# First expert gathers fed by GpSimd, rows in two column halves, one weight step moved ahead, and a residual write left out

## The reference

```python
def hierarchical_moe(hn, w_router_group, w_router_expert, w_gate, w_up, w_down):
    g_probs = softmax(t @ w_router_group); g_w, g_idx = top_k(g_probs, 1)
    e_in_group = (t @ w_router_expert)[group g_idx]          # 4 groups of 8 experts
    top_l, top_i = top_k(e_in_group, 2); weights = softmax(top_l) * g_w
    for e in range(32):
        hid = silu(t @ w_gate[e]) * (t @ w_up[e])            # 2048 -> 256
        out = out + (hid @ w_down[e]) * comb[:, e:e + 1]     # 256 -> 2048
```

## Time and profile before

| what | value |
|---|---|
| median of the runs | 2225.68 us (2225.47 to 2228.48, 3 runs) |
| the profiled execution's own time | 2228.09 us |
| its span | 2226.3 us |
| PE busy | 2156.8 us, 97% of the span |
| DVE busy | 1315.8 us, 59% |
| ACT busy | 900.7 us, 40% |
| POOL busy | 15.6 us, 1% |
| share of the chain that ended last | PE 83%, DMA 10%, DVE 4%, ACT 2% |
| moved | 520.49 MB, 234 GB/s over the span |

### The profile page before, as it was taken

One profiled execution on the slowest core, in us unless ns is written; L12 is line 12 of the kernel. 1 busy time (PEld: TensorE's weight loads), 2 busy tenths in 40 slices (PEclk: granted clock), 3 DMA queues, 4 the chain that ended last, 5 costly groups with the idle time before them and its releaser, 6 DMA issues.

```text
span 2226.3 us, 31966 instructions
## 1 busy us (share of the span) xinstructions
PE 2156.8 (97%) x12035; PEld 1699.3 (76%) x12035; DVE 1315.8 (59%) x1788; ACT 900.7 (40%) x1188; POOL 15.6 (1%) x30
## 2 busy tenths in 40 slices
PE   9999999999899888999999999999999999999998
PEld 8888888555445445888888888888888888888886
DVE  7797566422222224766667665777777777764443
ACT  4564455411111112554435454554434343433342
POOL 1000000000000000000000000000000000000000
PEclk9999999999999999999999999999999999999999
DMA  7765455899999998556654545546656556565653
GB/s 252 216 202 152 133 187 209 351 419 421 421 421 421 421 421 341 179 175 214 211 173 162 162 157 185 168 154 189 189 188 188 188 188 188 188 209 191 196 191 131
DMA packets 283474, 520.49 MB, mean 234 GB/s; under 512 B 22065, under 2 KB 194145, under 8 KB 258529
## 3 DMA queue, kind: packets, MB, share of 16 engines
q1 hardware_dynamic: 280560, 507.60, 65.2%
q0 software_dynamic: 2800, 11.34, 1.5%
HBM read 514.63 MB, written 7.36 MB: 234 GB/s over the span
## 4 chain that ended last, share of the span: by engine, by line
PE 83%; DMA 10%; DVE 4%; ACT 2%; issue 1%; SPq 0%; DVEq 0%; ACTq 0%
PE acc L723 30%; PE acc L744 24%; PE acc L747 12%; DMA mw<-in_w_expert_up 7%; PE ps L1168 5%; PE acc L1243 3%; DMA mw<-in_w_expert_gate 2%; DVE wlo L1977 1%; PE tp L832 1%; DMA mw_late<-in_w_expert_up 1%; PE ps L900 1%; PE tp L1126 1%; PE tp L1116 0%; PE ps L847 0%; PE tp L915 0%
## 5 line engine op out<-in xcount | busy, mean ns | idle before, releaser
L1977 DVE TENSOR_TENSOR wlo<-raw,whi 128x1024 fp32r<-128x1024 f32 x572 | 675.7, 1220 | 210.7 <-ACT whi L1461 206.2
L744 PE MATMUL acc<-xhl,whi 128*128 128x512 f32 x2496 | 790.6, 398 | 1.6 <-DVE wlo L1977 0.7
L1461 ACT ACTIVATE whi<-raw 128x1024 fp32r<-128x1024 f32 x572 | 582.1, 1053 | 351.9 <-DMA raw<-in_w_down 132.4
L747 PEld LDWEIGHTS acc<-xhl,wlo 128*128 128x128 f32 x2496 | 468.9, 188 | 110.8
L747 PE MATMUL acc<-xhl,wlo 128*128 128x256 f32 x2496 | 490.8, 278 | 0.0
L744 PEld LDWEIGHTS acc<-xhl,whi 128*128 128x128 f32 x2496 | 381.4, 189 | 5.8 <-issue 3.0
L1168 PE MATMUL ps<-mw,xg_turn 128*64 128x256 f32 x1536 | 177.2, 384 | 29.0 <-DMA mw<-in_w_expert_gate 22.1
L1168 PEld LDWEIGHTS ps<-mw,xg_turn 128*64 128x64 f32 x1536 | 112.0, 138 | 97.6 <-issue 27.0
L723 PE MATMUL acc<-whi,xhl 128*128 128x512 f32 x480 | 155.8, 395 | 0.0
L723 PE MATMUL acc<-whi,ah 128*128 128x512 f32 x336 | 130.7, 389 | 0.0
L723 PE MATMUL acc<-wlo,ah 128*128 128x512 f32 x336 | 130.7, 389 | 0.0
(11 more groups left out here) (457 smaller groups left out, 2394.7 us busy)
## 6 DMA issues: line engine op xcount, KB each, us to landing
raw<-in_w_in SPq DMA_DIRECT2D x352, 256.0 KB, 3.0
raw<-in_w_up SPq DMA_DIRECT2D x352, 256.0 KB, 2.9
mw<-in_w_expert_up SPq DMA_DIRECT2D x52, 1024.0 KB, 17.2
mw<-in_w_expert_gate SPq DMA_DIRECT2D x50, 1024.0 KB, 18.0
mw<-in_w_expert_down SPq DMA_DIRECT2D x48, 1024.0 KB, 18.2
raw<-in_w_down SPq DMA_DIRECT2D x176, 256.0 KB, 3.3
raw<-in_w_out SPq DMA_DIRECT2D x128, 256.0 KB, 3.2
raw<-in_w_ple_gate SPq DMA_DIRECT2D x64, 256.0 KB, 3.4
```

The costliest lines, as they stand in the source:

```text
L744: pe.matmul(out(ct).rearrange("p (m n) -> p m n", m=2), wh[:, ct * P:ct * P + P], ahl[:, :, k, :], start=first, stop=False, skip_group_che ...
L747: mm = pe.matmul(out(ct)[:, S:2 * S], wl[:, ct * P:ct * P + P], ahl[:, 0, k, :], start=False, stop=last, skip_group_check=True)
L1461: act.activation(whi[:, m % RING, :], raw[:, m % RING, :], ACT.Copy).then_inc(hi_ready, 1)
L1977: dve.tensor_tensor(wlo[:, m % RING, :], raw[:, m % RING, :], whi[:, m % RING, :], ALU.subtract).then_inc(lo_ready, 1)
```

## The change

ScalarE no longer makes `x_hi` for the first eight column groups. It writes the scaled rows themselves (`scaled_rows`) into space of `upb` that is still free, the first tile ahead of its wait for the router product. GpSimd copies them to `x_hi` (rounding to float32r) and subtracts to get `x_lo`. `x_hi` and `x_lo` hold eight column groups instead of sixteen; the second half is written over the first once eight gathers are done, by ScalarE (`high_rows`) and VectorE (`low_rows(1)`, now behind `slots_ready`). TensorE does eight gathers ahead of the first `gate_up`, followed by twelve small products without a use (`run_in`), and the other eight after the second `gate_up`. LATE no longer overlaps the rows, so step 6 goes there and is requested directly after step 2. The write of `h` to DRAM goes, and the overflow branch starts from `xp` and `g_pack` instead. Two scratch tiles move.

```diff
-OV_PE, OV_ACT, OV_DVE = 10, 1, 9
-OV_X = KT // 2
+OV_PE, OV_ACT, OV_DVE = 13, 1, 10
+OV_X = 1
+OV_IN = 96
 MAX_OVER = 7
+RUN_IN_MOE = 12
 EARLY, LATE = 4, 5
-PLACE = [EARLY, 0, 1, 2, 3, EARLY, 0, LATE, 1, 2, 3]
-PLACE += [PLACE[6 + (s - 6) % 5] for s in range(len(PLACE), N_STEPS)]
+PLACE = [EARLY, 0, 1, 2, 3, EARLY] + [(LATE, 0, 1, 2, 3)[s % 5] for s in range(N_STEPS - 6)]
...
-        junk_ra = at("junk_ra", 57, [P, 1536])
-        junk_la = at("junk_la", 63, [P, 512])
+        junk_ra = at("junk_ra", 26, [P, 1536])
+        junk_la = at("junk_la", 18, [P, 512])
...
-        x_lo = at("x_lo", 33, [P, TT, KT, P], F32R)
-        x_hi = at("x_hi", 49, [P, TT, KT, P], F32R)
+        upb_rows = at("x_scaled_rows", 73, [P, TT, D])
+        x_lo = at("x_lo", 33, [P, TT, KT // 2, P], F32R)
+        x_hi = at("x_hi", 41, [P, TT, KT // 2, P], F32R)
+        ov_w = at("ov_w", 33, [P, KT, P])
+        ov_gt = at("ov_gt", 65, [P, PACK // P, S])
+        ov_hid = at("ov_hid", 69, [P, PACK // P, 256])
+        x_part = [upb_rows[:, 1 - t, 1024:2048].rearrange("p (k q) -> p k q", k=8) for t in range(TT)]
...
@@ -470,8 +472,6 @@
                 earlier = [q for q in range(step) if PLACE[q] == r]
                 if earlier:
                     sp.wait_ge(w_used, earlier[-1] + 1)
-                elif r == LATE:
-                    sp.wait_ge(t_done, KT)
                 else:
                     sp.wait_ge(chunk_used, ND_MOE if r in (2, 3) else ND_MOE - 4)
                 m = 4 // len(sources)
@@ -479,14 +479,17 @@
                     dst = ring_w[r][:, m * j:m * j + m, :].rearrange("p a b -> p (a b)")
                     sp.dma_start(dst, w[e, :, m * c * CHUNK:m * (c + 1) * CHUNK]).then_inc(w_in_g[r], 16)
 
+            def pair_step(g, i):
+
+                c = i if g else FIRST_PAIR[i]
+                load_step(STEPS * g + i, [((wgp, wup)[c // 2], e, c % 2) for e in (2 * g, 2 * g + 1)])
+
             for g in range(PAIRS):
                 for i in range(4):
-                    c = i if g else FIRST_PAIR[i]
-                    load_step(STEPS * g + i, [((wgp, wup)[c // 2], e, c % 2) for e in (2 * g, 2 * g + 1)])
+                    if STEPS * g + i != STEPS:
+                        pair_step(g, i)
                     if g == 0 and i == 2:
-                        sp.wait_ge(acc_free[0], MIX_END[0])
-                        sp.wait_ge(acc_free[1], MIX_END[1])
-                        sp.dma_start(h_d, h[:, :, :]).then_inc(h_out, 16)
+                        pair_step(1, 0)
                 for j in range(2):
...
+            for t in range(TT):
+                pool.wait_ge(x_scaled, t + 1)
+                pool.tensor_copy(x_hi[:, t, :, :], x_part[t]).then_inc(xh_ready, 1)
+                pool.wait_ge(xh_ready, t + 1)
+                pool.tensor_tensor(x_lo[:, t, :, :], x_part[t], x_hi[:, t, :, :], ALU.subtract).then_inc(xl_ready, 1)
...
                 for m in range(2 * TT):
-                    mm = pe.matmul(o[:, :], x_k[m // TT][:, m % TT, kt, :], g_pack[:, m % TT, :], start=m == 0,
+                    mm = pe.matmul(o[:, :], x_k[m // TT][:, m % TT, kt % 8, :], g_pack[:, m % TT, :], start=m == 0,
                                    stop=m == 2 * TT - 1, skip_group_check=True)
...
-                    pe.wait_ge(ov_x, TT)
-                    for k in range(KT // 2):
-                        if k >= 2:
-                            pe.wait_ge(ov_act, k - 1)
-                        for j in range(2):
-                            for t in range(TT):
-                                x_t = h_was[:, t, :].rearrange("p (q k) -> p k q", k=KT)
-                                mm = pe.transpose(tp[k % 2][:, j * S + t * P:j * S + (t + 1) * P], x_t[:, 2 * k + j, :], ident[:, :])
-                        mm.then_inc(ov_pe, 1)
-                    pe.wait_ge(ov_act, KT // 2)
+                    for q in range(PACK // P):
+                        for t in range(TT):
+                            mm = pe.transpose(tp[q // 2][:, q % 2 * S + t * P:q % 2 * S + (t + 1) * P],
+                                              g_pack[:, t, q * P:(q + 1) * P].bitcast(F32), ident[:, :])
+                    mm.then_inc(ov_pe, 1)
+                    pe.wait_ge(ov_act, 2)
                     with pe.Fori(0, count) as i:
-                        for m in range(2):
-                            pe.wait_ge(ov_in, i * 48 + (16 * m + 16))
-                            for ht in range(2):
+                        for m in range(4):
+                            o = ((ps[0], ps[1]), (acc[1][:, 0:512], acc[1][:, 512:1024]))[m // 2]
+                            pe.wait_ge(ov_in, i * OV_IN + (16 * m + 16))
+                            for q in range(PACK // P):
+                                c = q % 2 * 256 + m % 2 * P
                                 for k in range(KT):
-                                    mm = pe.matmul(ps[m][:, ht * S:(ht + 1) * S], ov_w[:, k, ht * P:(ht + 1) * P], xT[:, k, :],
+                                    mm = pe.matmul(o[q // 2][:, c:c + P], xp[:, k, q * P:(q + 1) * P], ov_w[:, k, :],
                                                    start=k == 0, stop=k == KT - 1, skip_group_check=True)
                         pe.wait_ge(ov_dve, i * OV_DVE + 1)
+                        for m in range(2):
+                            for q in range(PACK // P):
+                                mm = pe.matmul(tp[0][:, m * S:(m + 1) * S], ov_hid[:, q, m * P:(m + 1) * P], ov_gt[:, q, :],
+                                               start=q == 0, stop=q == PACK // P - 1, skip_group_check=True)
+                        mm.then_inc(ov_pe, 1)
...
             pe.wait_ge(packed_ready, 1)
-            for kt in range(11):
+            for kt in range(8):
                 gather(kt)
+            run_in(RUN_IN_MOE)
...
                 gate_up(g, 0)
                 gate_up(g, 1)
                 if g == 0:
-                    for kt in range(11, KT):
+                    for kt in range(8, KT):
                         gather(kt)
...
+            act.wait_ge(n_inv, rows.n)
+
+            def high_rows(half, t):
+
+                act.activation(x_hi[:, t, :, :], h[:, t, :].rearrange("p (q k) -> p k q", k=KT)[:, 8 * half:8 * half + 8, :], ACT.Copy,
+                               scale=rstd2[:, 1, t:t + 1]).then_inc(xh_ready, 1)
+
+            def scaled_rows(t):
+
+                act.activation(x_part[t], h[:, t, :].rearrange("p (q k) -> p k q", k=KT)[:, 0:8, :], ACT.Copy,
+                               scale=rstd2[:, 1, t:t + 1]).then_inc(x_scaled, 1)
+
+            scaled_rows(0)
             act.wait_ge(rt_mm, 1)
             act.activation(lgT[:, :], ps[0][:, 0:S], ACT.Copy).then_inc(rt_copy, 1)
...
-            act.wait_ge(n_inv, rows.n)
-            for half in range(2):
-                ks = slice(8 * half, 8 * half + 8)
-                for t in range(TT):
-                    act.activation(x_hi[:, t, ks, :], h[:, t, :].rearrange("p (q k) -> p k q", k=KT)[:, ks, :], ACT.Copy,
-                                   scale=rstd2[:, 1, t:t + 1]).then_inc(xh_ready, 1)
-                embedded(half)
+            scaled_rows(1)
+            embedded(0)
+            embedded(1)
             act.wait_ge(rt_read, 2)
             act.activation(g_e[:, :, :], g_sh[:, :, :], ACT.Exp).then_inc(rt_e, 1)
             act.wait_ge(rt_read, 3)
             act.activation(r_s[:, 7, :], r_s[:, 6, :], ACT.Exp).then_inc(rt_e, 1)
+            act.wait_ge(xl_ready, TT)
             embedded(2)
             embedded(3)
...
                 copies(xg_first[half], first, slice(8 * half, 8 * half + 8))
+                if half == 0:
+                    act.wait_ge(t_done, 8)
+                    for t in range(TT):
+                        high_rows(1, t)
...
-            def low_rows(half):
-
-                ks = slice(8 * half, 8 * half + 8)
-                for t in range(TT):
-                    dve.wait_ge(xh_ready, TT * half + t + 1)
-                    dve.scalar_tensor_tensor(x_lo[:, t, ks, :], h[:, t, :].rearrange("p (q k) -> p k q", k=KT)[:, ks, :],
-                                             rstd2[:, 1, t:t + 1], x_hi[:, t, ks, :], ALU.mult, ALU.subtract).then_inc(xl_ready, 1)
-
-            low_rows(0)
             each = [P, TT, N_EXPERTS]
             dve.wait_ge(rank_mm, 1)
...
-            low_rows(1)
+            def low_rows(half):
+
+                for t in range(TT):
+                    dve.wait_ge(xh_ready, TT * half + t + 1)
+                    dve.scalar_tensor_tensor(x_lo[:, t, :, :], h[:, t, :].rearrange("p (q k) -> p k q", k=KT)[:, 8 * half:8 * half + 8, :],
+                                             rstd2[:, 1, t:t + 1], x_hi[:, t, :, :], ALU.mult, ALU.subtract).then_inc(xl_ready, 1)
+
...
             dve.sem_inc(slots_ready, 1)
+            low_rows(1)
...
-                if g == 1:
-                    dve.wait_ge(h_out, 16)
```

(3 more changed lines are left out.)

62 lines of the change are left out of this document (29 added, 33 removed).

## The result

| | before | after |
|---|---|---|
| median | 2226.84 us (2225.47 to 2228.77, 7 runs) | 2234.77 us (2231.39 to 2238.01, 7 runs) |
| the profiled execution, its span | 2228.09, 2226.3 us | 2231.39, 2229.6 us |

The changed kernel is slower: ratio 1.0035, 95% interval [1.0026, 1.0044], some 8 us. The forecast of 2225.5 us was wrong, and the time lies above its range. The profiled execution of the changed kernel is the shortest of its runs, that of before lies above its median, so the two traces differ by only 3.3 us.

A forecast was written before the change was run, and what follows sets the result against it. Bound by TensorE's chain from the router to its seventh weight step, then the weight stream. 2.2 us won less 2.06 paid left 0.1: 2228.0 us, or 2225.5 as median; own range 2222.6 to 2227.4, with rivals to 2231.9.

The forecast's parts named there:

- (3): GpSimd's four row instructions beside the router: about 8 us, done at 388.4 us, within a cover of 12.9 us, costing nothing.
- rival A: VectorE's two-input router operations stand still while GpSimd reads SBUF: 5.4 us delay, 2231.0 us in all; chance 0.37.
- (1): Low rows off VectorE between `taken` and the ranks: first gather at 393.3 instead of 395.47 us, 2.2 us won.
- (4): Eight gathers, then twelve run_in products (1.3 us) inside a 2.06 us copy wait; first gate_up at 402.8 us, 2.9 earlier.
- (5): Second-half rows and eight late gathers: third gate_up at 419.4 against 419.62 us, so 0.1 to 0.2 us remain.
- (2): ScalarE's scaled rows: two instructions of 2.0 us replace four, the first in a 2.42 us wait; cost nothing.
- (6): Sixth weight step requested ahead and no write of `h` (2048 KB): worth nothing.
- (7): Overflow branch not taken, its larger body jumped over as before; TensorE's idle time ahead of the last pair stays 3.5 us.
- (B): Rival: GpSimd's rows take 16 us, beyond the upper bound; gathers 3.0 us later, 2228.6 us; chance 0.06.
- (C): Rival: bytes count after all, so the dropped write's 5.0 us come off the end, 2220.6 us; chance 0.04.
- (D): Rival: the jump over the overflow branch gets cheaper, 4.2 us go, 2221.3 us; chance 0.06.
- step 11: Weight request at 443.7 us, after the seventh gate_up step; the stream is gapless from there, so its shift reaches the end.

The follow-up runs named there:

- e5: The changed kernel plus 20 filler products on TensorE ahead of its wait for `taken`; median 2231.6 us, ratio 1.0013 to the kernel before.
- b4: The kernel before with only TensorE's new order: eight gathers, filler, two gate_ups, eight gathers; median 2229.3 us, ratio 1.0009.
- b1: The kernel before with one high row made ahead of ScalarE's wait and its low row in VectorE's gap; median 2226.2 us, ratio 0.9989.
- e6: The changed kernel with the write of `h` and the sixth weight transfer's old turn brought back; median 2233.1 us, ratio 1.0028 to the kernel before.
- e4: The changed kernel with rows made by ScalarE and VectorE again, while GpSimd runs eight unused memsets; median 2230.0 us, ratio 1.0013 to the kernel before.
- b2: b1 plus nine filler products on TensorE ahead of the third gate_up; median 2224.5 us, ratio 0.9985 to the kernel before.
- e1: The changed kernel unaltered, run again for a second trace; median 2234.2 us, ratio 1.0029 to the kernel before.
- e2: The changed kernel without GpSimd's part, rows made by ScalarE and VectorE again; median 2230.0 us, ratio 1.0008 to the kernel before.
- b3: b1 with the five late gathers put between the first two gate_ups; median 2226.4 us, ratio 0.9995 to the kernel before.

## Why the prediction was wrong

**The step that failed is (3)**, in which GpSimd's four instructions cost nothing because they are done within their cover ("The cover is 12.9 us; beyond it each us is one"). Their duration was right enough: four instructions of 1.04, 2.41, 1.04 and 2.39 us, from 379.03 to 386.02 us, 7.0 us with 8 taken; and the rows were in time. (The Trainium skill, "GPSIMD Engine Reference", section 3.1, with what section 4, "When to use GPSIMD", says of one input, had led to an estimate of 6.5 to 7 us; the trace agrees.) The cover was for whoever waits for GpSimd's result. What it cost fell on whoever worked beside it, and VectorE's router is the head of the chain: its three stretched operations made `taken` 4.45 us late, which the sum had at nothing. This was rival A, with its mechanism, its place and nearly its size: 5.4 us of delay forecast, 4.45 measured, because GpSimd, which began where it was expected (R + 6.2 against 6.3), took 1 us less. It was given 0.37 against 0.42, on the ground that no row showed it; no row of a trace without GpSimd could have. The rule of the Trainium skill, cited beside it, should have outweighed rows that could say nothing either way.

**(1) The low rows.** They did come off, but the 2.2 us were not won as reckoned: from ranks to first gather it is 7.2 us against 8.2. Two embedding blocks fill them, the first partly at the lower clock. With that dip away (e5) it is 5.7 us: 2.5 us won, 1.5 of it lost to the clock behind the wait that (3) made.

**(4) The filler was mis-sized.** A product of the filler is two records: 24 records, 2.84 us, not 12 x 0.11 = 1.3. The row it rested on, "x32", counted records. It ends 0.6 us after the copies (405.93 + 1.16 = 407.09 against the gate_up's 407.64). First gather to first gate_up is 10.03 us, not 9.5, and no gain over the 10.20 of before.

**(5) The second half** went as reckoned: 16.7 us from first to third gate_up, forecast 16.6. So without any stall the change would have had 2.2 to 2.5 us to win and 2.7 to pay (b4), and b1 shows that over half of what was to win (1.3 us) could be had without paying.

**(2), (6), (7)** held: ScalarE's rows cost nothing (2.14 and 2.09 us, the first done 0.41 us ahead of `lgT`), the write and the order next to nothing (e6), the jump idles 3.64 us against 3.50. With that the other rivals fall: GpSimd took 7.0 us, not 16 (B), the bytes of the write don't show (C), the jump isn't cheaper (D). That step 11 sets the end held too: 4.7 us late at the stream's start, 4.6 at its end.

**The size of the whole.** Rival A had 2231.0 us, 5.3 more than before; measured were 7 to 8 more. Up to the third gate_up the delay of 6.0 us adds up: 4.45 from the stall, 2.7 from the second half, less 1.0 won behind the ranks and 0.2 in the first half. From there to the seventh step the clock decides: before lost 3.0 us to its dips (20.5 against the 17.5 of e4 and b2), the changed kernel 1.7 in its first trace, which is its shortest execution, and 4.6 in e1's. So the first trace is 4.6 us later at the end and e1's 8.3, and the medians lie between. The mean clock of the 13 executions of the changed kernel was 0.993 to 0.996, that of before's 103 was 0.996 or more in 83. That a longer idle time begets such a dip is shown in e5, for one place; why the dips beyond the third gate_up come in some executions and not in others stays open.

## What to carry to other kernels

Work given to an idle GpSimd isn't free by being off the path: look at what VectorE does in that time, and if that has two SBUF inputs and stands on the path, count as delay nearly all the time from its first such operation to the end of GpSimd's work (here 4.45 of 386.02 - 380.82 = 5.2 us), or let GpSimd only write. Before moving work to another engine, look for the few tenths in which the engines already there wait: one high row and one low row put into such gaps won some 2 us where four instructions on GpSimd lost 3 to 4. And a gain on the compute side reaches the end only if the transfer queue lets it: the gathers between the gate_ups were worth nothing until two transfers changed places, and then some 4 us.

## What the runs showed of the hardware

- A two-input operation of 8 columns on VectorE, both inputs in SBUF, that begins beside a reading GpSimd instruction ends 0.02 to 0.04 us after that instruction, three times of three in each of five kernels. With one of its two inputs in PSUM (`lg`) it took its 0.23 us; a reduce begun 0.02 us before GpSimd's subtraction took its 0.16 us.
- Beside memsets one VectorE operation was longer: the TENSOR_SCALAR of 0.17 us took 0.32 us and ended at 382.41 us, where by 8.04 / 8 = 1.005 us each the third memset ends, at 382.42. One case; a contention of writes, perhaps.
- GpSimd takes 1.04 us for a copy of 128x1024 in fp32 and 2.4 us for a subtraction, VectorE 1.22 us for one.
- The same idle time of 2.06 us ahead of the third gate_up was followed by 5.3 to 5.4 us for it in before, the changed kernel, e1, e6, b1 and b4, and by 3.67 us in e2 to e5, where the `down` products behind it were longer instead or nothing was: the clock's fall isn't tied to one idle time alone.
- The last weights landed 407.8 to 408.4 us after the start of the seventh step in 13 of 14 traces; in b3, whose DMA engines had stood idle for 2.6 us between 415 and 420 us, 410.5 us.
